# Delta-rule inverse: 8x8 diagonal blocks by back substitution in place of two product levels

## The chip, the cores and the metric

The kernel runs on one core of one Trainium2 chip. The metric is device microseconds of one execution, the median of three runs.

## The reference

Four residual layers over x (512 tokens x 1024): a gated DeltaNet, a gated ConvFFN, a differential attention, a second ConvFFN, each followed by a LayerNorm. What matters here is the DeltaNet's chunked delta rule, for each of 8 heads of width 128:

```python
low = jnp.where(strict, jnp.einsum('nbhid,nbhjd->nbhij', kb, k) * decay, 0.0)
a_mat = low + jnp.eye(C, dtype=f32)
rhs = jnp.concatenate([v * beta[..., None], kb * jnp.exp(gc)[..., None]], -1)
sol = lax.linalg.triangular_solve(a_mat, rhs, left_side=True, lower=True, unit_diagonal=True)
```

Then a scan over the chunks updates the state S and gives the output o, which is RMS-normalized, gated and projected. The kernel works with chunks of 128 tokens (NT = 4 of them) and forms the inverse T of the unit lower triangular matrix explicitly.

## The kernel before

Every engine has its own instruction list, written out by hand; the lists meet in semaphores. `PE_AT`, `DVE_AT`, `ACT_AT` and `POOL_AT` number the events of one head on each engine, and `pe("kk")`, `dve("L")`, `act("DT")`, `pool("TT")` wait for them; `own(...)` on an engine waits for an earlier result of its own. The DeltaNet's heads run one after the other (`step`, once on each engine; heads 0 to 5 in a loop over pairs, 6 and 7 unrolled, 7 with `more=False`). The parity e of the head picks one of two sets of buffers and three PSUM banks `X(e, 0..2)`.

Large products have float32 accuracy by three single products of high and low halves (`block_products`: L1449, L1450, L1451). While TensorE works on head h it also projects head h+1: 4 weight chunks (gate, q, k, v) x 8 contraction blocks = 32 fill units of three matmuls of 512 columns. `fill(p0, p1)` lays them between the small products of the head. In head 7 the fill is the output product instead (`mixer_unit`, 6 matmuls, L1437 to L1439), 14 units spread over the same 32 places. Each weight chunk (512 KB by DMA into one of two `raw` slots) is split by ScalarE (`split_hi`, L323) and VectorE (`split_lo`, L328) into one of four slots; `hold_hi` and `hold_lo` do it for the output weights kept aside. A raw slot is loaded again when its split is done.

The inverse T of a 128x128 block (four at once, one per chunk): L = k k^T scaled by the decays (L1083); T starts as the identity plus the negated sub-diagonal of the 2x2 blocks (VectorE L1085, L1087), its transpose TT the same from LT (GpSimd L552, L555). Then six levels s = 2, 4, 8, 16, 32, 64. In each, TensorE forms P = LT x T (`four`, L1505, 4 matmuls of 128 columns), VectorE masks it into PB (L1066), TensorE multiplies by TT for T's update and by PB for TT's (`part`, L1512, 4 matmuls of 64 columns each), and VectorE adds the updates (L1076, L1079). The last level updates TT alone. These products are in plain float32, for which the trace has two records per matmul. Between a level's first product and the others stand 2 fill units, 3 in level 2.

The order on TensorE in a head: 8 fill units, k k^T (event kk), k q^T (qk), k transposed (kt), 1 unit, L transposed (lt), 2 units, v transposed (vt, L1503, waits for `A`, the scaled q k^T, L1090), 1 unit, the levels, the recurrence over the four chunks with the state `S` (VectorE L1136, L1139) and the copies `v0` to `v3` (ScalarE), the last fill units, and the mean of squares (ms, L1593). Beside it ScalarE makes the decay factors DD, DT, ER (L682 to L689) from the row broadcast by a 256 KB DMA, and copies LT; GpSimd makes QD (L546), masks A (L549), then TTa and TT. VectorE does the convolution taps of the next head (`tap`, L1033, three per tensor, which free bank 0 or 1), the norms of q and k (L1041), and at the end o1, og, hi, lo of the finished head (L1150 to L1156).

Of the kernel before, what the change touches and what calls it, by code (L numbers as in the profile page):

```python
# [38 lines left out]
P = 128  # L39
# [20 lines left out]
LEVELS = [2, 4, 8, 16, 32, 64]  # L60
# [38 lines left out]
LV = [f"{k}{s}" for s in LEVELS for k in ("P", "T", "TT") if (k, s) != ("T", LEVELS[-1])]  # L99
PE_AT, PE_N = numbered(["kk", "qk", "kt", "lt", "vt"] + LV  # L100
                       + ["v0", "w", "S0", "v1", "S1", "v2", "S2", "v3", "o", "ms"])
DVE_AT, DVE_N = numbered(["L", "T0a", "T0", "A", "Rw", "kd", "Rv"] + LV + ["S0", "S1", "S2", "o1", "og", "hi", "lo"])
ACT_AT, ACT_N = numbered(["DDr", "DTr", "DD", "DT", "er", "LT", "v0", "w", "v1", "v2", "v3", "sq", "ln", "rms"])
POOL_AT, POOL_N = numbered(["qd", "mA", "TTa", "TT"])
# [24 lines left out]
def build(nc, a):  # L129
    ctx = ExitStack()  # L130
    with ctx:
# [24 lines left out]
        level = sb("level", [P, 7, P])  # L156
        level1T = sb("level1T", [P, P])
# [200 lines left out]
        def _(sp):  # L358
# [120 lines left out]
        def _(pool):  # L479
# [26 lines left out]
            made(nc.gpsimd.memset(level[:, :, :], 0.0))  # L506
            for i, s in enumerate([1] + LEVELS):

                v = level[:, i, :].rearrange("p (b h j) -> p b h j", h=2, j=s)[:, :, 0, :]
# [3 lines left out]
            made(nc.gpsimd.memset(level1T[:, :], 0.0))  # L513
            select(level1T[:, :].rearrange("p (b h) -> p b h", h=2)[:, :, 1], ALU.not_equal, -1.0, 0,
                   [[-2, P // 2]], 1)

# [19 lines left out]
            with pool.Fori(0, PAIRS) as it:  # L536
                for e in BOTH:
                    h = 2 * it + e
                    own = 1 + h * POOL_N
# [56 lines left out]
        def _(act):  # L596
# [73 lines left out]
            def step(h, e, more):  # L670
# [8 lines left out]
                act.wait_ge(row_loaded, 16 * h + 16)  # L679
# [15 lines left out]
                if more:  # L695
                    gate(h + 1, 1 - e)
                split_hi(act, C_GDN_IN, h, 7)
# [22 lines left out]
                if more:  # L720
                    split_hi(act, C_GDN_IN, h, 9)
                    tap(h + 1, 3)
# [19 lines left out]
            split_hi(act, C_GDN_IN, 0, 5)  # L742
            tap(0, 3)
# [179 lines left out]
        def _(dve):  # L923
# [56 lines left out]

            dve.wait_ge(params_loaded, 16 * N_PARAMS)
# [61 lines left out]

            def step(h, e, more):
# [49 lines left out]
                pe("vt")  # L1094
                nc.vector.tensor_tensor(RV[e][:, :, :], v3(X(e, 1)), bc(beta), ALU.mult).then_inc(d_dve, 1)
                split_lo(dve, C_GDN_IN, h, 6)
                if not more:
                    split_lo(dve, C_GDN_IN, h, 7)
                masked(0)
                added(0)  # L1100
                if more:
                    split_lo(dve, C_GDN_IN, h, 7)
                else:
                    hold_lo(dve, C_GDN_OUT + 4)
                masked(1)
                if more:
                    tap(h + 1, 1, 0)
                added(1)
                if more:
                    tap(h + 1, 1, 1)  # L1110
                masked(2)
                if more:
                    tap(h + 1, 1, 2)
                added(2)
                if not more:
                    hold_lo(dve, C_GDN_OUT + 5)
                masked(3)
                added(3)
                masked(4)
                added(4)  # L1120
# [4 lines left out]
                masked(5)  # L1125
                added(5)
# [811 lines left out]
```

## Time and profile before

| | us |
|---|---|
| median of 3 runs (lowest, highest) | 1574.72 (1572.68, 1575.71) |
| profiled execution: its time, its span | 1572.31, 1570.5 |
| busy in the span: PE, DVE, ACT, POOL | 1469.8, 869.2, 626.1, 130.3 |
| heads of the delta rule, first k k^T to the last ms | 67.47 to 481.18 |
| starts of k k^T in heads 0, 1, 6, 7 | 67.47, 118.08, 377.33, 435.11 |

The profile is of one execution. A row of busy time by stretch lists PE, PEld, DVE, ACT and POOL in this order. PE is the matrix engine (TensorE), PEld its weight loads, DVE VectorE, ACT ScalarE, POOL GpSimd. Matmuls overlap, so the distance between two starts tells what one costs, not its duration. A row's bracket says how long the engine was idle before it and what it waited for. "Clock" is the share of TensorE's full clock that was granted.

### The profile page before, as it was taken

To read this page: it belongs to the slowest core of one execution; us is meant where nothing else is said; L and a number is where in the kernel's file an instruction comes from. 1 tells how busy PE (TensorE), PEld (TensorE's weight loads), DVE (VectorE), ACT (ScalarE), POOL (GpSimd) and SP (SyncE) were. 2 spreads that over 40 slices of the span, in tenths; PEclk is the share of its full clock that TensorE was granted. 3 is DMA by queue.
4 is the path that set the end of the run, shared out by engine and by line. 5 is a ranking of instruction groups with operands and counts; after the bars stand their busy time and mean duration, and the time that the engine had idled before them with its cause. 6 is when DMAs were issued, how large, how long until landed. Compare 5 with 4: busy or idle time off the path is not lost.

```text
span 1570.5 us, 20997 instructions
## 1 busy us (share of the span) xinstructions
PE 1469.8 (94%) x7474; PEld 1204.3 (77%) x7474; DVE 869.2 (55%) x1288; ACT 626.1 (40%) x997; POOL 130.3 (8%) x121
## 2 busy tenths in 40 slices
PE   6899999999889699999999999999996999999997
PEld 5688778887777678888788777677676788887886
DVE  5556655666455466666522544777755666665225
ACT  4743554345422244444411224565522444444220
POOL 4101110111012000000000201111020000000002
PEclk8999999999999899999999999999998999999999
DMA  5211111111120133333322131112211333333321
GB/s 165 57 52 48 47 46 40 47 47 47 41 68 14 54 95 95 104 93 93 134 101 101 44 104 54 41 54 80 83 38 54 97 96 101 93 93 134 107 95 67
DMA packets 157726, 118.85 MB, mean 76 GB/s; under 512 B 5898, under 2 KB 145644, under 8 KB 157676
## 3 DMA queue, kind: packets, MB, share of 16 engines
q1 hardware_dynamic: 157676, 118.17, 24.6%
q8 instruction: 33, 0.54, 0.1%
q14 instruction: 17, 0.14, 0.0%
HBM read 116.04 MB, written 2.11 MB: 75 GB/s over the span
## 4 chain that ended last, share of the span: by engine, by line
PE 76%; DVE 10%; ACT 5%; issue 4%; POOL 2%; DMA 2%; SPq 1%; ACTq 0%; DVEq 0%; POOLq 0%
PE bank L1449 13%; PE bank L1451 13%; PE bank L1450 13%; PE bank L1437 7%; PE bank L1439 7%; PE bank L1438 7%; PE bank L1512 5%; PE bank L1505 3%; DVE w_lo L328 1%; PE bank L1787 1%; PE bank L1805 1%; DVE x_tok L1184 1%; PE bank L1746 1%; DVE bn L1188 1%; DVE x_tok L1199 1%
## 5 line engine op out<-in xcount | busy, mean ns | idle before, releaser
L1449 PE MATMUL bank<-x_hi,w_hi 128*128 128x512 f32 (+1 forms) x1160 | 463.3, 399 | 29.3 <-DVE x_lo L938 25.8
L1451 PE MATMUL bank<-x_hi,w_lo 128*128 128x512 f32 (+1 forms) x1160 | 442.3, 381 | 0.0
L1450 PE MATMUL bank<-x_lo,w_hi 128*128 128x512 f32 (+1 forms) x1160 | 441.7, 381 | 0.0
L328 DVE TENSOR_TENSOR w_lo<-raw,w_hi 128x1024 fp32r<-128x1024 f32 x196 | 246.6, 1261 | 311.6 <-ACT w_hi L323 298.9
L1449 PEld LDWEIGHTS bank<-x_hi,w_hi 128*128 128x128 f32 x1160 | 223.4, 193 | 68.4 <-DVE w_lo L328 24.2
L323 ACT ACTIVATE w_hi<-raw 128x1024 fp32r<-128x1024 f32 x188 | 196.9, 1050 | 191.9 <-PE bank L1439 154.3
L1451 PEld LDWEIGHTS bank<-x_hi,w_lo 128*128 128x128 f32 x1160 | 222.4, 192 | 41.5
L1450 PEld LDWEIGHTS bank<-x_lo,w_hi 128*128 128x128 f32 x1160 | 223.5, 193 | 37.3 <-issue 3.4
L1437 PE MATMUL bank<-w_hi,u_hi 128*128 128x512 f32 x416 | 165.9, 399 | 14.3 <-issue 5.7
L1439 PE MATMUL bank<-w_hi,u_lo 128*128 128x512 f32 x416 | 163.7, 393 | 0.0
L1438 PE MATMUL bank<-w_lo,u_hi 128*128 128x512 f32 x416 | 163.5, 393 | 0.0
L1437 PEld LDWEIGHTS bank<-w_hi,u_hi 128*128 128x128 f32 x416 | 79.1, 190 | 33.6 <-issue 11.3
L1439 PEld LDWEIGHTS bank<-w_hi,u_lo 128*128 128x128 f32 x416 | 79.0, 190 | 16.8
L1438 PEld LDWEIGHTS bank<-w_lo,u_hi 128*128 128x128 f32 x416 | 79.1, 190 | 16.5 <-issue 0.5
L564 POOL TENSOR_TENSOR x_tok<-x_tok,gb 128x1024 f32<-128x1024 f32 x8 | 19.3, 2408 | 854.3 <-DVE x_tok L1204 854.3
L823 ACT ACTIVATE u_hi<-acc_b 128x512 f32 (+1 forms) x44 | 27.8, 632 | 116.0 <-DVE acc_b L1277 116.0
L650 ACT ACTIVATE scr<-bank,vec 128x512 f32<-128x512 f32 x24 | 16.4, 684 | 116.7 <-PE bank L1451 116.7
L1033 DVE SCALAR_TENSOR_TENSOR scr<-bank,vec,scr 128x511 f32<-128x511 f32 (+2 forms) x72 | 53.6, 745 | 9.3 <-ACT scr L650 5.4
L820 ACT ACTIVATE acc_a<-acc_a 128x512 f32<-128x512 f32 x44 | 27.8, 632 | 77.6 <-DVE acc_a L1272 77.6
L1269 DVE SCALAR_TENSOR_TENSOR acc_b<-bank,vec,acc_b 128x511 f32<-128x511 f32 x44 | 33.0, 749 | 39.0 <-ACT acc_b L816 39.0
L816 ACT ACTIVATE acc_b<-bank,vec 128x512 f32<-128x512 f32 x44 | 34.2, 777 | 49.7 <-PE bank L1451 49.7
L1280 DVE TENSOR_TENSOR u_lo<-acc_b,u_hi 128x512 f32 (+1 forms) x44 | 30.5, 692 | 39.9 <-ACT u_hi L823 39.9
(268 smaller groups left out, 1925.6 us busy)
## 6 DMA issues: line engine op xcount, KB each, us to landing
raw<-in_ffn_w_up SPq DMA_DIRECT2D x88, 512.0 KB, 3.7
raw<-in_ffn_w_down SPq DMA_DIRECT2D x44, 512.0 KB, 3.2
raw<-in_gdn_w_in SPq DMA_DIRECT2D x32, 512.0 KB, 4.1
raw<-in_diff_w_in SPq DMA_DIRECT2D x24, 512.0 KB, 3.7
raw<-in_gdn_w_out SPq DMA_DIRECT2D x8, 512.0 KB, 3.3
raw<-in_diff_w_out SPq DMA_DIRECT2D x8, 512.0 KB, 3.3
x_tok<-in_x SPq DMA_DIRECT2D x4, 512.0 KB, 5.7
ROW<-decay_rows SPq DMA_DIRECT2D x8, 256.0 KB, 4.6
```

The costliest lines, as they stand in the source:

```text
L323: nc.scalar.activation(w_hi[:, s, :], raw[:, (base + r) % RAW, :], ACT.Copy).then_inc(hi_ready, 1)
L328: nc.vector.tensor_tensor(w_lo[:, s, :], raw[:, (base + r) % RAW, :], w_hi[:, s, :].bitcast(F32), ALU.subtract).then_inc(lo_ready, 1)
L816: nc.scalar.activation(acc, b[:, :], ACT.Identity, bias=fcb(l, t), scale=fcw(l, 2, t)).then_inc(f_act, 1)
L1033: ins = nc.vector.scalar_tensor_tensor(acc[:, sh:T], bank[r % 2][:, 0:T - sh], gcw(3 - sh, i * 8 + h), acc[:, sh:T], ALU.mult, ALU.add)
L1437: nc.tensor.matmul(out, hi[:, k, tok], high[:, cols], start=(k == 0), stop=False)
L1438: nc.tensor.matmul(out, hi[:, k, tok], low[:, cols], start=False, stop=False)
L1439: ins = nc.tensor.matmul(out, lo[:, k, tok], high[:, cols], start=False, stop=(k == K - 1))
L1449: nc.tensor.matmul(out, hi, x_hi[:, k, cols], start=(k == 0), stop=False)
L1450: nc.tensor.matmul(out, hi, x_lo[:, k, cols], start=False, stop=False)
L1451: ins = nc.tensor.matmul(out, lo, x_hi[:, k, cols], start=False, stop=last)
L1505: ins = nc.tensor.matmul(out, lhsT(n), rhs(n), start=True, stop=True)
L1512: ins = nc.tensor.matmul(halves(X(e, i)[:, c], s, h), lhsT[e][:, n, :], halves(rhs[e][:, n, :], s, h), start=True, stop=True)
```

## The change

The lowest levels are replaced by a direct solve. T's 8x8 diagonal blocks are found by back substitution: L is masked to its 8x8 diagonal blocks with a minus sign (`Lb`), a reduction packs the 16 blocks of a row into 8 columns (`Lc`, 128 x 4 x 8), a broadcast product with `place_in` (which column in its block a partition has) lays row m of each block in its own 8 columns (`R`, 128 x 256), and one float32 product with `same` (ones where two tokens share a block) spreads each row to all partitions of its block (`bc`, 256 columns, into bank `X(1-e, 2)`). VectorE then solves for m = 7 down to 1 in 13 small operations on `Tc` (128 x 4 x 8), and a last one writes T (`T0`). TT comes from T by four transposes on TensorE (`tt`) and a copy on ScalarE. Levels 2 and 4 and GpSimd's TTa and TT are gone. v is transposed behind level 8's first product, into `X(1-e, 2)`. The fill is cut anew: 7, 2, 2, 5, 1, 2 units, then as before. The weight splits move: each head does chunks 7 to 10 counted from its own first one, instead of 6 to 9; chunk 6 is split before head 0, and chunks 9 and 10 earlier in the head, ahead of the third tap. Head 7's second output unit no longer waits for all of head 6 but for its event `ln`. The row loads get a semaphore per parity.

```diff
-LEVELS = [2, 4, 8, 16, 32, 64]
+BASE = 8
+NB = P // BASE
+LEVELS = [8, 16, 32, 64]
...
@@ VectorE, before the heads
+            dve.wait_ge(masks_ready, 2)
+            nc.vector.tensor_reduce(place_in[:, :], ident[:, :].rearrange("p (b j) -> p j b", j=BASE), AX.X,
+                                    ALU.add).then_inc(place_ready, 1)
...
+            split_lo(dve, C_GDN_IN, 0, 6)
             norms(0, 0)
...
@@ GpSimd, in a head
-                    pool.wait_ge(d_act, from_act + ACT_AT["LT"])
-                    nc.gpsimd.tensor_tensor(TT[e][:, :, :], LT[e][:, :, :], rep(level1T[:, :]),
-                                            ALU.mult).then_inc(d_pool, 1)
-                    pool.wait_ge(d_pool, own + POOL_AT["TTa"])
-                    nc.gpsimd.tensor_tensor(TT[e][:, :, :], TT[e][:, :, :], rep(ident[:, :]),
-                                            ALU.add).then_inc(d_pool, 1)
...
@@ ScalarE, in a head
                 nc.scalar.activation(LT[e][:, :, :], v3(X(e, 0)), ACT.Copy).then_inc(d_act, 1)
-                split_hi(act, C_GDN_IN, h, 6)
                 if more:
+                    split_hi(act, C_GDN_IN, h, 7)
                     gate(h + 1, 1 - e)
-                split_hi(act, C_GDN_IN, h, 7)
+                    tap(h + 1, 1)
+                pe("tt")
+                nc.scalar.activation(TT[e][:, :, :], v3(X(e, 1)), ACT.Copy).then_inc(d_act, 1)
...
                 if more:
-                    tap(h + 1, 1)
                     silu(h + 1, 1 - e, 1)
                     split_hi(act, C_GDN_IN, h, 8)
+                    split_hi(act, C_GDN_IN, h, 9)
                     tap(h + 1, 2)
+                    split_hi(act, C_GDN_IN, h, 10)
...
                 if more:
-                    split_hi(act, C_GDN_IN, h, 9)
                     tap(h + 1, 3)
...
+            split_hi(act, C_GDN_IN, 0, 6)
             tap(0, 3)
...
@@ VectorE, the solve
+                rows_of = X(1 - e, 2)[:, 0:NT * BASE * BASE].rearrange("p (n m j) -> p n m j", m=BASE, j=BASE)
+                dve.wait_ge(d_pe, 1 + h * PE_N + PE_AT["bc"])
+                nc.vector.scalar_tensor_tensor(Tc[:, :, :], rows_of[:, :, BASE - 1, :], place_in[:, BASE - 1:BASE],
+                                               place_in[:, :].unsqueeze(1).to_broadcast([P, NT, BASE]), ALU.mult,
+                                               ALU.add).then_inc(d_dve, 1)
+                before = "c0"
+                for m in range(BASE - 2, 0, -1):
+                    own(before)
+                    nc.vector.tensor_tensor(step_c[:, :, 0:m], rows_of[:, :, m, 0:m],
+                                            Tc[:, :, m:m + 1].to_broadcast([P, NT, m]), ALU.mult).then_inc(d_dve, 1)
+                    own(f"c{m}")
+                    nc.vector.tensor_tensor(Tc[:, :, 0:m], Tc[:, :, 0:m], step_c[:, :, 0:m], ALU.add).then_inc(d_dve, 1)
+                    before = f"a{m}"
...
@@ VectorE, in a head
-                own("T0a")
-                nc.vector.tensor_tensor(TM[e][:, :, :], TM[e][:, :, :], rep(ident[:, :]), ALU.add).then_inc(d_dve, 1)
+                own("Lb")
+                nc.vector.tensor_reduce(Lc[:, :, :], TM[e][:, :, :].rearrange("p n (b j) -> p n j b", j=BASE), AX.X,
+                                        ALU.add).then_inc(d_dve, 1)
+                own("Lc")
+                nc.vector.tensor_tensor(spread(e), Lc[:, :, :].unsqueeze(2).to_broadcast([P, NT, BASE, BASE]),
+                                        place_in[:, :].unsqueeze(1).unsqueeze(3).to_broadcast([P, NT, BASE, BASE]),
+                                        ALU.mult).then_inc(d_dve, 1)
                 pe("qk")
                 act("DT")
                 nc.vector.tensor_tensor(AT[e][:, :, :], v3(X(e, 1)), DT[e][:, :, :], ALU.mult).then_inc(d_dve, 1)
+                if not more:
+                    split_lo(dve, C_GDN_IN, h, 7)
+                solve(h, e)
+                own(SOLVE[-1])
+                nc.vector.tensor_tensor(TM[e][:, :, :].rearrange("p n (b j) -> p n b j", j=BASE),
+                                        Tc[:, :, :].unsqueeze(2).to_broadcast([P, NT, NB, BASE]),
+                                        same[:, :].rearrange("p (b j) -> p b j", j=BASE).unsqueeze(1).to_broadcast(
+                                            [P, NT, NB, BASE]), ALU.mult).then_inc(d_dve, 1)
...
+                masked(0)
                 nc.vector.tensor_tensor(KD[e][:, :, :], v3(X(e, 2)), bc(kdecs), ALU.mult).then_inc(d_dve, 1)
...
                 if more:
                     split_lo(dve, C_GDN_IN, h, 7)
+                    tap(h + 1, 1, 0)
+                added(0)
+                pe("vt")
+                nc.vector.tensor_tensor(RV[e][:, :, :], v3(X(1 - e, 2)), bc(beta), ALU.mult).then_inc(d_dve, 1)
+                if not more:
                     hold_lo(dve, C_GDN_OUT + 4)
...
@@ TensorE
-                                pe.wait_ge(d_act, 1 + (HEADS - 1) * ACT_N)
-                                pe.wait_ge(d_dve, D_DVE0 + (HEADS - 1) * DVE_N)
+                                pe.wait_ge(d_act, 1 + (HEADS - 2) * ACT_N + ACT_AT["ln"])
...
-                dve("A")
-                pe.wait_ge(in_act, 1 + IA_N * h + IA["v silu"])
-                four(1, cols(vT), None, turn=True)
-                fill(11, 12)
-                p = 12
+                dve("R")
+                nc.tensor.matmul(X(1 - e, 2)[:, 0:NT * BASE * BASE], same[:, :], TT[e][:, 0:2, :].rearrange("p a b -> p (a b)"),
+                                 start=True, stop=True).then_inc(d_pe, 1)
+                fill(11, 16)
+                p = 16
...
                     four(0, at(LT), at(TM))
...
                     if i == 0:
+                        four(1, at(TM), None, turn=True)
+                        fill(p, p + 1)
+                        p += 1
+                        pe.wait_ge(in_act, 1 + IA_N * h + IA["v silu"])
...
+                    fill(p, p + 2)
+                    p += 2
                     if i == 0:
-                        pool("TT")
-                        dve("Rv")
+                        dve("kd")
+                        act("TT")
```

## Rows read from the trace of the kernel before

**Rows 1.** Busy us by stretch: start:end, length, engines (instructions), clock, DMA share, GB/s.

```profile
67.47:118.08 50.61, 49.68 (x308) 41.75 (x309) 27.50 (x44) 23.80 (x44) 6.14 (x4) 1.00 0.18 47
169.85:221.79 51.94, 49.74 (x310) 41.61 (x309) 30.30 (x46) 24.07 (x45) 5.97 (x4) 1.00 0.17 45
377.33:422.36 45.03, 43.14 (x283) 36.66 (x282) 25.09 (x39) 17.67 (x33) 5.97 (x4) 1.00 0.12 42
422.36:435.11 12.75, 8.20 (x22) 5.44 (x21) 7.05 (x10) 11.46 (x23) 1.28 (x1) 0.73 0.12 41
435.11:481.18 46.07, 40.44 (x274) 35.64 (x272) 22.62 (x33) 9.61 (x14) 4.65 (x3) 1.00 0.21 69
```

**Rows 2.** Order of time, TensorE, head 2: start, us, engine, line, names, [idle].

```profile
171.64 0.60 PE L1503 MATMUL bank<-ident,kT 128*128 128x128 f32 x4
171.99 0.48 PE L1449 MATMUL bank<-x_hi,w_hi 128*128 128x512 f32 x1
...
175.82 0.65 PE L1503 MATMUL bank<-ident,vT 128*128 128x128 f32 x4 [1.05 <-DVE DT L1090]
...
180.65 1.10 PE L1512 MATMUL bank<-PB,TT 128*128 128x64 f32 x8 [0.52 <-POOL TT L555]
...
186.80 1.11 PE L1505 MATMUL bank<-TM,LT 128*128 128x128 f32 x8
187.67 0.47 PE L1449 MATMUL bank<-x_hi,w_hi 128*128 128x512 f32 x1
...
189.13 1.00 PE L1512 MATMUL bank<-PB,TT 128*128 128x64 f32 x8
...
190.86 1.11 PE L1505 MATMUL bank<-TM,LT 128*128 128x128 f32 x8
...
194.93 1.08 PE L1467 MATMUL bank<-sq_q,ones 128*128 128x512 f32 x2
195.85 1.05 PE L1505 MATMUL bank<-TM,LT 128*128 128x128 f32 x8
```

**Rows 3.** Order of time, VectorE, start of head 2.

```profile
172.67 0.69 DVE L1085 TENSOR_TENSOR TM<-DD,level 128x512 f32<-128x512 f32 x1
173.40 1.69 DVE L1087 TENSOR_TENSOR TM<-TM,ident 128x512 f32<-128x512 f32 x1
175.01 0.68 DVE L1090 TENSOR_TENSOR DT<-bank,DT 128x512 f32<-128x512 f32 x1
175.61 0.67 DVE L1092 TENSOR_TENSOR RW<-bank,bege 128x512 f32<-128x512 f32 x1
```

**Rows 4.** Order of time, GpSimd, the same stretch.

```profile
173.24 1.30 POOL L546 TENSOR_TENSOR QD<-qT,ER 128x512 f32<-128x512 f32 x1 [44.57 <-ACT ER L689]
175.77 1.29 POOL L549 TENSOR_TENSOR DT<-DT,upto 128x512 f32<-128x512 f32 x1 [1.23 <-DVE DT L1090]
```

**Rows 5.** Order of time, ScalarE, the same stretch.

```profile
171.73 1.26 ACT L689 ACTIVATE ER<-ROW,gmid 128x128 f32<-128x128 f32 x4
```

**Rows 6.** Order of time, VectorE's small operations before the heads.

```profile
35.65 0.19 DVE L987 TENSOR_TENSOR ab<-ab,heads_row 128x32 f32<-128x32 f32 x1
35.88 0.19 DVE L990 SCALAR_TENSOR_TENSOR ab<-ab 128x32 f32<-128x32 f32 x1
...
44.14 0.19 DVE L1004 COPY gcol<-bank 128x32 f32<-128x32 f32 x1 [2.72 <-ACT kdecs L640]
...
44.96 0.29 DVE L1016 TENSOR_REDUCE small<-lamp 128x2 f32<-128x128 f32 x1
```

**Rows 7.** Order of time, TensorE, at both ends of the heads.

```profile
67.47 1.16 PE L1505 MATMUL bank<-kT 128*128 128x128 f32 x8 [0.95 <-DVE kT L1041]
...
426.99 0.47 PE L1437 MATMUL bank<-w_hi,u_hi 128*128 128x512 f32 x1 [3.50 <-DVE scr L1033]
...
442.66 0.50 PE L1437 MATMUL bank<-w_hi,u_hi 128*128 128x512 f32 x1 [2.90 <-DVE w_lo L328]
```

**Rows 8.** The page's costliest groups: VectorE's weight split.

```profile
L328 DVE TENSOR_TENSOR w_lo<-raw,w_hi 128x1024 fp32r<-128x1024 f32 x196 | 246.6, 1261 | 311.6 <-ACT w_hi L323 298.9
```

More of the change, by code:

```diff
@@ L155, in build @@
         after = sb("after", [P, P])
-        level = sb("level", [P, 7, P])
-        level1T = sb("level1T", [P, P])
+        level = sb("level", [P, len(LEVELS) + 1, P])
+        same = sb("same", [P, P])
+        place_in = sb("place_in", [P, BASE])
+        Lc = sb("Lc", [P, NT, BASE])
+        Tc = sb("Tc", [P, NT, BASE])
+        step_c = sb("step_c", [P, NT, BASE])
         ones = sb("ones", [P, P])
@@ L505, in _ @@
             made(nc.gpsimd.memset(mean_h[:, :], 1.0 / P))
-            made(nc.gpsimd.memset(level[:, :, :], 0.0))
-            for i, s in enumerate([1] + LEVELS):
-                v = level[:, i, :].rearrange("p (b h j) -> p b h j", h=2, j=s)[:, :, 0, :]
+            made(nc.gpsimd.memset(same[:, :], 1.0))
+            v = same[:, :].rearrange("p (b j) -> p b j", j=BASE)
+            select(v, ALU.is_ge, 0.0, 0, [[-BASE, NB], [0, BASE]], 1)
+            select(v, ALU.is_ge, 0.0, BASE - 1, [[BASE, NB], [0, BASE]], -1)
+            made(nc.gpsimd.memset(level[:, 0, :], -1.0))
+            v = level[:, 0, :].rearrange("p (b j) -> p b j", j=BASE)
+            select(v, ALU.is_gt, 0.0, 0, [[-BASE, NB], [-1, BASE]], 1)
+            select(v, ALU.is_ge, 0.0, BASE - 1, [[BASE, NB], [0, BASE]], -1)
+            made(nc.gpsimd.memset(level[:, 1:, :], 0.0))
+            for i, s in enumerate(LEVELS):
+                v = level[:, i + 1, :].rearrange("p (b h j) -> p b h j", h=2, j=s)[:, :, 0, :]
                 made(nc.gpsimd.memset(v, -1.0))
@@ L538, in _ @@
                     h = 2 * it + e
-                    own = 1 + h * POOL_N
                     from_act = 1 + h * ACT_N
@@ L1042, in norms, with spread, solve, own @@
                                                    ALU.mult, ALU.mult).then_inc(in_dve, 1)
+            def spread(e):
+                return TT[e][:, 0:2, :].rearrange("p a (b m j) -> p (a b) m j", m=BASE, j=BASE)
+            def solve(h, e):
+                def own(name):
+                    dve.wait_ge(d_dve, D_DVE0 + h * DVE_N + DVE_AT[name])
+                rows_of = X(1 - e, 2)[:, 0:NT * BASE * BASE].rearrange("p (n m j) -> p n m j", m=BASE, j=BASE)
[11 more added lines that the diff above has]
+                    before = f"a{m}"
             def step(h, e, more):
@@ L1106, in step @@
                 if more:
-                    tap(h + 1, 1, 0)
+                    tap(h + 1, 1, 1)
                 added(1)
                 if more:
-                    tap(h + 1, 1, 1)
+                    tap(h + 1, 1, 2)
+                else:
+                    hold_lo(dve, C_GDN_OUT + 5)
                 masked(2)
[L1112 to L1120, printed above, removed]
                 if more:
@@ L1124, in step @@
                     hold_lo(dve, C_GDN_OUT + 6)
-                masked(5)
-                added(5)
+                added(2)
+                if more:
+                    split_lo(dve, C_GDN_IN, h, 9)
+                masked(3)
+                added(3)
                 if not more:
@@ L1136, in step @@
                         nc.vector.tensor_copy(S, new).then_inc(d_dve, 1)
+                        if more:
+                            split_lo(dve, C_GDN_IN, h, 10)
                     else:
@@ L1167, in _ @@
                 tap(0, 3, j)
+            split_lo(dve, C_GDN_IN, 0, 6)
             norms(0, 0)
+            dve.wait_ge(place_ready, 1)
+            dve.wait_ge(masks_ready, N_MASKS)
             with dve.Fori(0, PAIRS - 1) as it:
@@ L1522, in step @@
                 pe.wait_ge(d_dve, 1 + h * DVE_N)
-                fill(0, 8)
+                fill(0, 7)
                 pe.wait_ge(in_dve, 1 + ID_N * h + ID["k norm"])
@@ L1527, in step @@
                 four(2, cols(kT), None, turn=True)
-                fill(8, 9)
+                fill(7, 9)
                 dve("L")
@@ L1555, in step @@
                     part(2, PB, TT, s, 1)
-                    if more and s == LEVELS[3]:
+                    if more and s == LEVELS[2]:
                         square_sum(h + 1, 1 - e, 0)
```

46 lines of the change are left out of this document (21 added, 25 removed).

## The prediction

> **What bounds the kernel now.** I read the busy times by stretch first [rows 1]. The eight heads of the delta rule are the stretch from 67.47 to 481.18 us. Heads 1 to 5 take (377.33 - 118.08) / 5 = 51.85 us each, with TensorE busy 49.74 of 51.94 and its clock at 1.00; VectorE is busy 30.30, ScalarE 24.07, GpSimd 5.97. So a head costs what TensorE does in it (the head's small products, and 32 units of the next head's projection laid between them), plus short waits. TensorE's order of time [rows 2] gives the prices. K is the start of the products k k^T: 169.85 in the head shown. Four transposes cost 0.35 (171.64 to 171.99). One level costs 0.87 for LT x T (186.80 to 187.67) and 1.73 for its two halved products (189.13 to 190.86), so 2.60 without fill; two fill units between take 1.46, which is 0.78 for the first and 0.70 for each further one. Two waits stand out: 1.05 modelled before the v transposes (1.22 against an undisturbed pitch) and 0.52 modelled (0.68) before the first halved product, put down to GpSimd's TT. The VectorE, GpSimd and ScalarE rows [rows 3 to 5] show where they come from: ScalarE's exponentials ER end at 172.99, GpSimd's QD runs 173.24 to 174.54, VectorE's second mask step on T (L1087) has 0.69 us of work, yet occupies 173.40 to 175.09, that is until QD ends plus its own time; the scaled q k^T follows and then the v transposes. I read this as: a VectorE operation with two SBUF inputs and a GpSimd one exclude each other. In contrast L1092 (an input in PSUM) runs 0.67 beside GpSimd's 1.29 at 175.77.
>
> **TensorE, part by part.** Removed in each head: levels 2 and 4, 2 x 2.60 = 5.20. Gone with them: 1.22 before the v transposes (they move behind level 8's first product, where v has long been ready), 0.68 for GpSimd's TT, and 0.15 in level 4. Added: four transposes for TT, 0.35; and the product that spreads the rows. It has 256 columns. The square sum, same type, 512 columns, takes 0.92 (194.93 to 195.85 [rows 2]), so 0.46 and some 0.1 for the change of weights; bounds 0.46 and 0.92. The number of fill units stays 32, cut into 16 pieces instead of 17 (-0.08). Without new waits: 51.85 - 5.20 - 1.22 - 0.68 - 0.15 - 0.08 + 0.35 + 0.56 = 45.45.
>
> **The new waits.** I walk one head from K. K comes one unit (0.70) earlier against the ScalarE chain from the head before, as 7 units precede it and not 8; the third tap now stands ahead of the weight split, which gives 0.16 back. So ER ends at K + 3.14 + 0.54 = 3.68 and QD runs 3.93 to 5.23. TensorE: kk, qk and k transposes to 2.14, two units to 3.62, L transposes to 3.97, two units to 5.45: there it wants R, the spread operand. VectorE: L starts near 2.2, Lb 2.9, Lc 3.65, at the dependent pitch of 0.72 [rows 3]. Lc, a reduction of 512 elements, isn't in the trace; the 128-element one takes 0.29 [rows 6], so 384 elements more at the pace of the 512-element products give 0.65 to 0.7; upper bound 1.69, what L1087 took with GpSimd in its way. I take 0.7. R reads two SBUF tensors and waits for QD's end: 5.23 to 5.6. TensorE loses 0.2 (bounds 0 and 1.2) and starts the spread at 5.65, fill at 6.2, and its five units end at 9.8.
>
> Meanwhile VectorE scales q k^T (5.6 to 6.2) and GpSimd masks it from 0.76 after that start (175.01 to 175.77 [rows 3, 4]): 6.36 to 7.65. The spread's result is there at about 6.5, 0.84 after its start. Now the solve: 13 dependent small operations on at most 32 elements. The nearest rows [rows 6]: 128x32, dependent, 35.65 to 35.88, pitch 0.23 at a duration of 0.19; read from PSUM also 0.19. The operations shrink to 4 elements, so I take 0.22 each; bounds 0.15 (the duration less its elements) and 0.35 (a quarter more than the 128-element reduction's 0.29). c0 and c6 read PSUM and run to 6.94; a6 reads two SBUF tensors and waits for GpSimd until 7.65; eleven more end near 10.05; the product that writes T0 takes 0.69, so T0 stands at 10.75. TensorE waited 0.95 for it (bounds: 0 if nothing waits for GpSimd and the operations take 0.19; 2.6 at 0.35 each). A pitch that differs by 0.1 moves each head by 1.3.
>
> The Trainium skill speaks against this form: "VectorE: DVE Perf Modes", section "The TRN2 errata — SBUF-src ops pay a fixed extra latency per instruction", gives each instruction a fixed cost, which many small tiles pay each time, and 62 cycles (65 ns) more for a PSUM source. By it the seven operations that read the spread rows cost 0.45 a head more and the kernel would end 3.6 later, near 1537; the row of the 32-element copy from PSUM (0.19, as from SBUF) doesn't agree, and I go by the row. The same skill's "SBUF — State Buffer", section "Who interferes with whom", has tensor_reduce never contend with GpSimd; if the trace holds otherwise, QD starts up to 0.4 late behind Lc and so does the rest; no row of before shows a long reduction.
>
> **The rest of a head.** Level 8 starts at x = K + 10.75. VectorE does RW (0.6), level 8's mask (from x + 1.15), KD to x + 2.4; ScalarE's copy of TT is done by x + 2.1; TensorE has 0.87 + 0.35 + 0.78 + 0.35 + 1.48 = 3.8 before it needs them: hidden. The split of chunk 7 and the first tap end by x + 4.2, before the T8 product ends. Further on the covers are thinner: the split of chunk 8 waits for ScalarE, which now does the silu and square of the new q just before; it ends near x + 14.5, and T32's addition stands behind it, wanted at x + 14.55. I charge 0.3; bounds 0 and 1.5 (both splits late by one 1.2). The splits of chunks 9 and 10 move before and behind S0, whose waits in the trace are VectorE waiting for TensorE. Each head still issues four 512 KB loads and one 256 KB row, now in some 46.7 us instead of 51.9: 51 GB/s instead of 45 [rows 1]. The row load of two heads on is queued behind load 12 and waits for v3 of this head, while the next weight load wants a split of the next head: nothing is held. GpSimd loses TTa and TT, which also frees the split that they slowed. Sum: 45.45 + 0.2 + 0.95 + 0.3 = 46.9; the walk, by 10.75 to level 8 and 35.96 from there to the next K, has 46.7. I take 46.7, a gain of 5.15.
>
> **The ends.** Head 0 (50.61 [rows 1]) lacked the 1.22, but ER is early, so neither R nor a6 waits: 45.85, gain 4.75. Head 6 up to its mean of squares: 45.03 becomes 40.5, gain 4.5. The passage to head 7, 12.75, has a 3.50 wait for the taps [rows 7], then a wait for head 6's last instruction, and a clock of 0.73. The taps now run before the split (1.2 earlier) and the second wait is only for ScalarE's logarithm. So 3.4, and three units of the output product at 1.39: 7.6, gain 5.2, at full clock. Head 7 (46.07): -5.20 for the levels, -2.9 for the split that TensorE waited for [rows 7], +0.91 for the added products, +0.9 for T0, +1.4 for the first held weight split, which VectorE now reaches behind TT8 and RV, when TensorE has used its fill: gain 5.0. Against this, the split of chunk 6 moved ahead of head 0: VectorE has k normalized at 67.41, TensorE waited 0.95 for it [rows 7]; one split of 1.26 [rows 8] and ScalarE's own stand before it now. Bounds 1.1 and 2.3, I take 1.6. That makes TensorE idle for 3.1 there; behind the idle 3.5 at 423.5 the clock fell, with 13 matmuls 0.2 longer each. I charge one such fall, 2.6 (bounds 0 and 5.2, for one at either end). The reduction for place_in stands in the chain of gates at 35 us: 0.25.
> Sum: 4.75 + 5 x 5.15 + 4.5 + 5.2 + 5.0 - 1.6 - 2.6 - 0.25 = 40.75. The profiled execution took 1572.31 (span 1570.5); the median of the three others is 2.4 higher. 1574.72 - 40.75 = 1534.0. All after 481 us (1,089 us) is not touched.
>
> **The rivals.** (a) The solve is hidden: operations at 0.19, the GpSimd mask out of the way, no clock fall. 1.15 a head and 2.6: 1534.0 - 9.2 - 2.6 = 1522. For it: VectorE is idle 20 us in a head. Against: the mask's start is tied to VectorE's own product just before. 12 in 100. (b) The small operations cost 0.35: 13 x 0.13 = 1.7 a head, 1547.5. For it: seven of them read a strided PSUM pattern with a broadcast, which no row shows. Against: the durations barely depend on the size. 17 in 100. (c) VectorE's queue becomes the limit inside the levels, as each addition that TensorE wants stands behind a split or a tap: 1.2 a head more, 1543.5. The first levels of before show that 0.15 is lost behind a split. 10 in 100. (d) Slower: the wait before T0 makes the clock fall in every head. The idle 3.5 did that, 1.05 a head doesn't. From 0.42 an operation the wait is 3.5 and the fall costs 2.6 more, which together is the whole gain of a head; at 0.50 it is 3.6 + 2.6 = 6.2 a head, and the time 1584. Speaks against it: no small operation of the trace is near. 3 in 100. That the levels' products stay isn't possible: they are issued in one list. My forecast has 58 in 100.
>
> **Numbers.** Range 1523 to 1550: it takes in (a) but for its edge, (c) and (b). Faster by over 0.2% (3.1 us, about what can be told from no change here) 0.95, within it 0.02, slower 0.03.
>
> **What would show it.** Right: from K to K 46.7, some 270 matmuls a head in place of 310; R ends just after QD; a6 long, about 0.9, and its eleven followers near 0.22 apart; TensorE's wait before level 8 about 1 us; no wait before the v transposes. Wrong: a wait of 2 or more before level 8 or a clock under 1.00 inside the heads (b, d); waits before levels 16 to 64 put down to T (c); the start of head 0's products earlier than 68.5 or later than 70.5.

## The result: 1530.3 us, 44 us less, and the profile after

The changed kernel's median is 1530.31 us (four runs, 1526.78 to 1533.51) beside 1574.45 before; the ratio is 0.972 with a 95% interval of 0.9696 to 0.9744. Forecast were 1534.0 and a range of 1523 to 1550. The profiled execution took 1530.73, its span is 1529.0 instead of 1570.5: 41.5 less. All of it lies in the heads: the last mean of squares starts at 439.56 instead of 481.18, 41.6 earlier, and the rest takes 1089.4 as against 1089.3.

Busy us by stretch after the change (columns as in [rows 1]): head 0, head 4, head 6 to its mean of squares, the passage to head 7, and head 7.

```profile
70.57:117.89 47.32, 46.49 (x266) 38.81 (x267) 27.52 (x52) 23.64 (x41) 2.62 (x2) 0.96 0.24 67
256.76:303.12 46.36, 44.98 (x267) 37.21 (x266) 30.24 (x56) 24.94 (x45) 2.60 (x2) 1.00 0.19 51
349.36:389.75 40.39, 39.17 (x245) 32.77 (x243) 26.08 (x49) 19.78 (x35) 2.59 (x2) 1.00 0.16 53
389.75:398.79 9.04, 6.79 (x21) 4.85 (x21) 6.01 (x9) 8.54 (x20) 0.00 (x0) 0.81 0.00 1
398.79:439.56 40.77, 36.22 (x231) 31.13 (x230) 21.13 (x41) 11.16 (x18) 3.47 (x2) 1.00 0.21 65
```

Against [rows 1]: head 0 has 47.32 instead of 50.61; heads 1 to 5 (117.89 to 349.36) have 46.29 on average instead of 51.85; then 40.39 for 45.03, 9.04 for 12.75, 40.77 for 46.07. TensorE has 44.98 busy of 46.36 in head 4 and 267 matmul records instead of 310. VectorE's busy time is as before (30.24): what it lost in levels it got back in the solve. GpSimd's falls from 5.97 to 2.60, with two operations left of four. The clock stays at 1.00 inside head 4; it is under 1 in head 0 and in the passage.

TensorE in head 4, from the spread product (L1583) to level 64, answering to [rows 2]:

```profile
262.28 0.70 PE L1583 MATMUL bank<-TT,same 128*128 128x256 f32 x2
262.63 0.58 PE L1500 MATMUL bank<-x_hi,w_hi 128*128 128x512 f32 x1
...
267.10 1.16 PE L1555 MATMUL bank<-TM,LT 128*128 128x128 f32 x8 [0.67 <-DVE TM L1140]
268.09 0.60 PE L1553 MATMUL bank<-ident,TM 128*128 128x128 f32 x4
268.45 0.47 PE L1500 MATMUL bank<-x_hi,w_hi 128*128 128x512 f32 x1
...
269.23 0.60 PE L1600 MATMUL bank<-ident,vT 128*128 128x128 f32 x4
...
280.89 1.08 PE L1518 MATMUL bank<-sq_q,ones 128*128 128x512 f32 x2
282.04 1.16 PE L1555 MATMUL bank<-TM,LT 128*128 128x128 f32 x8
```

The same stretch on VectorE and on GpSimd, answering to [rows 3, 4]. L1127 is the packing reduction, L1130 the spread operand R, L1072 c0, L1078 the products and L1081 the additions of the solve, L1140 writes T0.

```profile
260.29 1.13 DVE L1127 TENSOR_REDUCE Lc<-TM 128x32 f32<-128x512 f32 x1
261.45 0.78 DVE L1130 TENSOR_TENSOR TT<-Lc,place_in 128x256 f32<-128x256 f32 x1
262.15 0.68 DVE L1135 TENSOR_TENSOR DT<-bank,DT 128x512 f32<-128x512 f32 x1
263.02 0.25 DVE L1072 SCALAR_TENSOR_TENSOR Tc<-bank,place_in 128x32 f32<-128x32 f32 x1 [0.19 <-PE bank L1583]
263.31 0.18 DVE L1078 TENSOR_TENSOR step_c<-bank,Tc 128x24 f32<-128x24 f32 x1
263.52 0.73 DVE L1081 TENSOR_TENSOR Tc<-Tc,step_c 128x24 f32<-128x24 f32 x1
264.29 0.18 DVE L1078 TENSOR_TENSOR step_c<-bank,Tc 128x20 f32<-128x20 f32 x1
...
266.15 0.17 DVE L1081 TENSOR_TENSOR Tc<-Tc,step_c 128x4 f32<-128x4 f32 x1
266.35 0.69 DVE L1140 TENSOR_TENSOR TM<-Tc,same 128x512 f32<-128x512 f32 x1
```

```profile
260.65 1.29 POOL L561 TENSOR_TENSOR QD<-qT,ER 128x512 f32<-128x512 f32 x1 [42.78 <-ACT ER L698]
262.91 1.30 POOL L564 TENSOR_TENSOR DT<-DT,upto 128x512 f32<-128x512 f32 x1 [0.96 <-DVE DT L1135]
```

Read the first addition of the solve: 0.73 us at 263.52, the next ones 0.18. It ends at 264.25, 0.04 behind the end of GpSimd's mask (262.91 + 1.30 = 264.21). R (L1130) takes 0.78 where QD (L561) is still running until 261.94. Since the solve ends late, T0 stands at 267.04. TensorE's last fill unit begins at 265.58, and at 0.68 for a unit the next product could have started at 266.26; it starts at 267.10. So TensorE loses 0.84, of which the row shows 0.67.

### The profile page after: what moved, and what is told of

Its sections match the earlier page's. It is cut to its first block, busy times and chain, and to the rows that moved or that the text cites. A ratio compares the mean times of both kernels' runs of the same rounds, so it can differ in the third digit from the quotient of the medians.

```text
span 1529.0 us, 20387 instructions
## 1 busy us (share of the span) xinstructions
PE 1430.5 (94%) x7138; PEld 1168.3 (76%) x7138; DVE 870.0 (57%) x1361; ACT 632.2 (41%) x1005; POOL 100.4 (7%) x100
## 4 chain that ended last, share of the span: by engine, by line
PE 79%; DVE 13%; ACT 3%; issue 2%; DMA 2%; SPq 1%; DVEq 0%; ACTq 0%
PE bank L1500 14%; PE bank L1502 14%; PE bank L1501 14%; PE bank L1488 7%; PE bank L1490 7%; PE bank L1489 7%; PE bank L1555 3%; PE bank L1562 2%; DVE w_lo L340 1%; PE bank L1845 1%; PE bank L1863 1%; PE bank L1804 1%; DVE x_tok L1235 1%; DVE bn L1239 1%; DVE x_tok L1250 1%
## 5 line engine op out<-in xcount | busy, mean ns | idle before, releaser
L340 DVE TENSOR_TENSOR w_lo<-raw,w_hi 128x1024 fp32r<-128x1024 f32 x196 | 239.7, 1225 | 304.8 <-ACT w_hi L335 292.4
L837 ACT ACTIVATE u_hi<-acc_b 128x512 f32 (+1 forms) x44 | 27.8, 632 | 116.0 <-DVE acc_b L1328 116.0
L834 ACT ACTIVATE acc_a<-acc_a 128x512 f32<-128x512 f32 x44 | 27.8, 632 | 78.0 <-DVE acc_a L1323 78.0
L830 ACT ACTIVATE acc_a<-bank,vec 128x512 f32<-128x512 f32 x44 | 34.2, 778 | 23.4 <-PE bank L1502 23.4
```

The source lines that it names most:

```text
L340: nc.vector.tensor_tensor(w_lo[:, s, :], raw[:, (base + r) % RAW, :], w_hi[:, s, :].bitcast(F32), ALU.subtract).then_inc(lo_ready, 1)
L830: nc.scalar.activation(acc, b[:, :], ACT.Identity, bias=fcb(l, t), scale=fcw(l, 2, t)).then_inc(f_act, 1)
```

## The experiments

Twelve experiments ran, one of them the changed kernel again. For those that ran several times the ratio is to the kernel before. A profile's total also varies outside the heads: from the last mean of squares to the end, code that no kernel touches, it is 1089.2 to 1094.6 in the fourteen profiles. So for one edit I go by the distance from one head's k k^T to the next's, which differs by 0.1 within a profile, and by the times only where they are many.

**1. GpSimd's mask behind the solve.**

```diff
-                    pool.wait_ge(d_dve, D_DVE0 + h * DVE_N + DVE_AT["A"])
+                    pool.wait_ge(d_dve, D_DVE0 + h * DVE_N + DVE_AT["T0"])
```

> The changed kernel, but GpSimd masks the scaled q k^T only when T0 is written. Theory (two-input VectorE operations and GpSimd's exclude each other): the first addition a6 falls from 0.73 to 0.18 us, so T0 is ready 0.55 earlier and TensorE's wait before level 8 falls from 0.67 modelled to about 0.1; from one head's k k^T to the next's 45.7 to 45.8 instead of 46.28; about 4.4 us in all. The mask then runs beside operations that read PSUM and is done before the next weight split. Rival (a6 is long for another reason, as the first addition or by its size): a6 stays at 0.73, heads stay at 46.28, time unchanged.

Heads take 45.69 to 45.82. The time is 1525.89 (four runs), ratio 0.9704 (0.9678 to 0.9730); the interval overlaps the changed kernel's, the heads don't. The additions of the solve, VectorE then GpSimd:

```profile
260.73 0.18 DVE L1078 TENSOR_TENSOR step_c<-bank,Tc 128x24 f32<-128x24 f32 x1
260.94 0.18 DVE L1081 TENSOR_TENSOR Tc<-Tc,step_c 128x24 f32<-128x24 f32 x1
261.16 0.18 DVE L1078 TENSOR_TENSOR step_c<-bank,Tc 128x20 f32<-128x20 f32 x1
```

```profile
264.00 1.27 POOL L564 TENSOR_TENSOR DT<-DT,upto 128x512 f32<-128x512 f32 x1 [4.63 <-DVE TM L1140]
```

The first addition is like the others. The theory holds and the rival falls.

**2 and 3. A longer solve.** Each product is issued three or five times, which leaves its result as it is.

```diff
-SOLVE = ["c0"] + [f"{k}{m}" for m in range(BASE - 2, 0, -1) for k in "ca"]
+SOLVE = ["c0"] + [f"{k}{m}" for m in range(BASE - 2, 0, -1) for k in [*(f"x{i}_" for i in range(AGAIN)), "c", "a"]]
```

> The changed kernel, with each of the six products of the solve issued three times (same result), so 25 small operations instead of 13. Theory (the solve lies on the path, its operations cost 0.21 each): 12 x 0.21 = 2.5 us a head more, the wait before level 8 becomes 3.2, heads 48.8, some 20 us in all, and no clock fall inside the heads. Rival (the solve is mostly hidden by fill and the wait has another cause): under 1 us a head. Rival d of the prediction (a long wait before level 8 lets the clock fall): granted clock under 1.00 in the heads and more than 3.5 us a head.

> The same with each product issued five times: 37 small operations. Theory: 24 x 0.21 = 5.0 us a head if the clock holds. The wait is then 5.7, longer than the 3.5 behind which the clock fell in the kernel before; so I expect a fall in each head, 13 to 15 matmuls 0.2 longer, 7.6 to 8 us a head, heads near 54, and so slower than the kernel before: about 1593. Rival (no fall, the clock goes by the whole head): 51.3 a head, 1571.

Two heads of the 25-operation kernel and the starts of their level 8, then two heads of the one with 37 and the start of level 8 in the second of them:

```profile
218.91:267.22 48.31, 44.86 (x268) 37.19 (x266) 31.80 (x68) 24.93 (x45) 2.60 (x2) 1.00 0.18 49
267.22:317.20 49.98, 46.56 (x268) 38.46 (x266) 31.86 (x67) 24.90 (x45) 2.58 (x2) 0.97 0.18 47
```

```profile
231.23 1.16 PE L1557 MATMUL bank<-TM,LT 128*128 128x128 f32 x8 [2.75 <-DVE TM L1142]
...
279.58 1.16 PE L1557 MATMUL bank<-TM,LT 128*128 128x128 f32 x8 [2.73 <-DVE TM L1142]
```

```profile
176.49:228.90 52.41, 46.58 (x268) 38.70 (x267) 33.85 (x80) 24.93 (x45) 2.59 (x2) 0.97 0.16 45
228.90:282.32 53.42, 47.59 (x267) 39.61 (x266) 33.75 (x80) 24.90 (x45) 2.60 (x2) 0.94 0.16 44
```

```profile
243.57 2.07 PE L1557 MATMUL bank<-TM,LT 128*128 128x128 f32 x8 [5.12 <-DVE TM L1142]
```

With 25 operations three of heads 1 to 5 take 48.31 to 48.37: 2.05 more for 12 operations. Twelve at 0.21 are 2.5; 0.42 of it is saved, as the first addition comes that much later and finds GpSimd further on (it takes 0.29 instead of 0.73). The time is 1552.1 in one run. The other two take 49.97 and 49.98, at a clock of 0.97, behind a wait of the same length (2.73 and 2.75). So a fall costs 1.65 there. I had expected none at this length; one length of wait gives both outcomes. With 37, heads 1 to 5 have 52.37 to 53.67 behind waits of 5.1 to 5.3, and the clock is never 1.00 but 0.97 or 0.94. In those heads level 8's first product already takes 1.97 to 2.08 us, so the clock is down when the wait ends; with 25 operations it takes 1.16 in all five heads, and where the clock falls, it does so behind it. From the first operation of the solve to T0 the 37 take 7.76 (235.06 to 242.82) and the 13 take 3.33 (263.02 to 266.35). Without a fall a head would have 46.29 + 4.43 = 50.7, so a fall costs 1.7 to 3.0. I had taken more for the longer operations and the fall together, and so the kernel took 1582.4 (one run) and not 1593. It is slower than the one before (1572.4 beside it): the prediction's slower case exists. But spread over the 13 operations, the 25 amount to 0.41 each (5.39 in all) and the 37 to 0.60, and at 0.41 a head still gains 1.9 to 3.5; I had put the point where the gain is gone at 0.42, so that case was further off than I had it.

**4. The packing reduction, in order of address.** This kernel leaves the packing out, so what it computes is no longer the inverse; it serves to price the reading alone.

```diff
-                nc.vector.tensor_reduce(Lc[:, :, :], TM[e][:, :, :].rearrange("p n (b j) -> p n j b", j=BASE), AX.X,
+                nc.vector.tensor_reduce(Lc[:, :, :], TM[e][:, :, :].rearrange("p n (j b) -> p n j b", j=BASE), AX.X,
```

> The changed kernel, with the reduction that packs the blocks reading its 512 elements in order of address (16 neighbours to a sum) instead of 16 elements 32 bytes apart; this leaves the packing out, so the inverse isn't the reference's. Strided reading as the cause of 1.1 us: falls to 0.7, as the 128-element one by its 0.29 in order and 0.38 strided. Rival (a reduction costs by its element count and groups alike): stays at 1.1. In both the heads keep 46.28, since the spread operand waits for GpSimd's QD.

One line's instructions (ns min/median/max), the changed kernel and this one:

```profile
L1127 DVE TENSOR_REDUCE Lc<-TM x8: 1093/1127/1189, 73.3 to 401.3; 128x32 f32<-128x512 f32 x8
```

```profile
L1127 DVE TENSOR_REDUCE Lc<-TM x8: 686/686/689, 72.8 to 397.6; 128x32 f32<-128x512 f32 x8
```

686 ns in order, 1127 strided by 32 bytes. The heads stay at 46.24 to 46.31 (1527.05 in one run), since R waits for QD in any case. The 0.7 that I had taken is the price of reading in order.

**5. The kernel before with GpSimd's work in another order**: TTa and TT, then the mask, QD last (four blocks moved, TensorE's wait for the last of them renamed).

> The kernel before with one edit: GpSimd does TTa and TT first, then the mask of A, and QD last. Theory (two of the terms of the forecast, 1.22 before the v transposes and 0.68 before the first halved product, belong to GpSimd's place in the head and not to the levels): L1087 falls from 1.69 to 0.69, the wait before the v transposes and the one for TT go, 1.3 to 1.9 us a head, heads 50.0 to 50.5 instead of 51.85, and 10 to 14 us in all, 1560. So about a third of the changed kernel's gain was to be had without the solve. Rival (those waits are put down wrongly and come from ScalarE's chain): they stay, under 3 us in all. Bounds for the case that QD, now last, becomes late for the recurrence: a wait at the product with QD, no gain.

Head 3 and head 7; VectorE's second mask step, TensorE's v transposes:

```profile
219.73:270.29 50.56, 49.68 (x309) 41.63 (x308) 28.80 (x46) 24.09 (x45) 5.90 (x4) 1.00 0.18 47
428.43:475.57 47.14, 41.74 (x274) 36.62 (x273) 22.38 (x33) 9.61 (x14) 6.99 (x4) 0.96 0.23 68
```

```profile
223.25 0.69 DVE L1087 TENSOR_TENSOR TM<-TM,ident 128x512 f32<-128x512 f32 x1
```

```profile
224.90 0.66 PE L1503 MATMUL bank<-ident,vT 128*128 128x128 f32 x4 [0.25 <-ACT vT L656]
```

Heads 1 to 5 take 50.39 to 50.58, 1.33 less, as expected, and L1087 has its 0.69. In all, though, the ratio is only 0.997 (0.9957 to 0.9984; ten runs, 1569.99 beside 1573.39), 3 to 5 us and not 10 to 14: I had multiplied by eight. In the profile heads 0 to 6 gain 8.5, but head 0 starts 1.12 later, the passage, which keeps its wait of 3.5, takes 13.48 instead of 12.75 at a clock of 0.62 instead of 0.73, and head 7 takes 47.14, 1.07 more than before, at a clock of 0.96. So 1.3 of a head's 5.56 was to be had without the solve.

**6. Six fill units ahead of level 8.**

```diff
-                fill(11, 16)
-                p = 16
+                fill(11, 17)
+                p = 17
```

(and one unit instead of two behind the v transposes)

> The changed kernel with six fill units instead of five between the spread product and level 8, one fewer behind the v transposes. Theory: the unit (0.70) covers the wait of 0.67 before level 8; the place it leaves needs KD and TT only 2.4 us after level 8's start and has 3.1 left; heads 45.6 to 45.7 instead of 46.28. Rival (TensorE then waits for KD or TT): heads 46.0 to 46.3 with a wait before level 8's first halved product.

```profile
252.14:297.78 45.64, 44.94 (x267) 37.20 (x266) 30.21 (x55) 24.92 (x45) 2.58 (x2) 1.00 0.19 52
```

Heads 1 to 5 take 45.55 to 45.64 (1524.4 in one run). The unit covers the wait and is free where it was taken from: the theory holds.

**7. Chunk 6's split behind head 0's norms.**

```diff
-            split_hi(act, C_GDN_IN, 0, 6)
             tap(0, 3)
             norm_exp(0, 0)
             norm_exp(0, 1)
+            split_hi(act, C_GDN_IN, 0, 6)
```

(and on VectorE, `split_lo` behind `norms`)

> The changed kernel with chunk 6's split behind the norms of head 0 on both engines instead of ahead of the third tap and of the norms. Theory: k is normalized 1.1 to 1.5 earlier, the wait before head 0's first products falls from 3.17 to 1.7 to 2.1. At that length the clock may hold (it fell behind 2.75 in two of five heads of the 25-operation kernel and held behind 1.05), which would make head 0 45.8 to 46.3 instead of 47.32. Rival (ScalarE's decay factors, one split later now, are then the last in head 0): L waits for DD, a wait before the L transposes of up to 1.

The first product of head 0, the changed kernel and this one, and this one's head 0:

```profile
70.57 1.16 PE L1555 MATMUL bank<-kT 128*128 128x128 f32 x8 [3.17 <-DVE kT L1058]
```

```profile
66.27 1.16 PE L1555 MATMUL bank<-kT 128*128 128x128 f32 x8 [1.69 <-DVE kT L1058]
```

```profile
66.27:112.82 46.55, 45.16 (x266) 37.29 (x267) 29.62 (x53) 25.12 (x46) 2.61 (x2) 1.00 0.25 69
```

The wait is 1.69 instead of 3.17, the clock 1.00, head 0 takes 46.55 instead of 47.32. L did wait for ScalarE (1.08 on VectorE), hidden by fill. Head 7's mean of squares starts 4.86 earlier than in the first profile of the changed kernel, and 1.66 earlier than in its second (experiment 10), where the clock fell neither at 54.7 nor in the passage. The one profile's total was 1530.0 all the same: its rest took 1093.6. The three kernels with this edit (7, 9 and 12) have the three longest rests, 1093.5 to 1094.6, the others 1089.2 to 1092.4; why, I haven't tried, so whether the edit itself gives some of its gain back there stays open.

**8. Blocks of 4 instead of 8**: `BASE = 4`, `LEVELS = [4, 8, 16, 32, 64]`, three fill units in place of five, two in the new level.

> The changed kernel with 4x4 diagonal blocks: a solve of 5 small operations, and level 4 back, with its two fill units. Theory (a level costs TensorE 2.60, the small operations only what they leave uncovered): + 2.60 for the level, - 0.1 to 0.2 for the narrower spread product (64 columns), and the wait before level 4 from 0.67 to 0.3 to 0.5, as 8 operations less (1.7) stand against two fill units less (1.4) and the mask of A still blocks: heads 48.4 to 48.8, some 19 us slower than the changed kernel. Rival (a dropped level is worth less than its products since other waits fill the place): heads under 47.8.

```profile
217.57:266.69 49.12, 47.26 (x291) 39.79 (x290) 30.56 (x50) 24.84 (x45) 2.60 (x2) 1.00 0.18 48
```

```profile
225.96 1.16 PE L1557 MATMUL bank<-TM,LT 128*128 128x128 f32 x8 [0.47 <-DVE TM L1140]
...
230.82 1.10 PE L1564 MATMUL bank<-PB,TT 128*128 128x64 f32 x8 [0.75 <-ACT TT L710]
```

49.1 to 49.3, 1552.0 in one run: 2.9 a head for the level, more than the 2.1 to 2.5 expected. The 0.47 before level 4 was expected; the 0.75 wasn't: ScalarE's copy of TT stands behind the tap of chunk 1, and chunk 1 is projected only with unit 16, which now comes later. The rival (under 47.8) falls. Without that 0.75, which comes of where the copy stands, the level would cost a head some 2.2 (an estimate from these rows), less than the 2.60 of its products, since the solve of 4x4 blocks is shorter and its spread product narrower. So what a dropped level is worth with the copy well placed isn't shown.

**9, 10 and 12. Edits 1, 6 and 7 together; the changed kernel again; and the three edits with QD behind T0 too.**

```diff
                     pool.wait_ge(in_dve, 1 + ID_N * h + ID["q norm"])
+                    pool.wait_ge(d_dve, D_DVE0 + h * DVE_N + DVE_AT["T0"])
```

> The changed kernel with three edits at once: the mask of A behind T0, six fill units ahead of level 8, chunk 6's split behind the norms. Each alone: heads 45.75, 45.58, and head 0's start 4.3 earlier (66.27). The first two hide the same wait, so heads 45.4 to 45.6, not 45.0; head 0 45.5 to 46, start 66.3 to 68.6. Sum against the changed kernel: 5 x 0.7 + 1 + 2 to 4, 6 to 9 us: 1521 to 1524. Rival (the gains of the start are lost again in the rest, as one profile had it): 1526.

> The changed kernel as it is, beside the one with three edits: 1530 plus or minus 2, ratio to before 0.972 to 0.974. Heads 46.3; the start and the passage to head 7 differ with the clock's falls by up to 2 us each.

> The three edits and GpSimd's QD behind T0 as well. Theory: R is no longer held (0.78 becomes 0.43), the spread product starts with TensorE's own pace, 0.08 to 0.15 earlier; with the mask ending 2.6 behind T0 the split of chunk 7 is held by some 0.2, covered. Heads 0.1 lower than with three edits. Rival (QD late for the recurrence or the split of chunk 7 holding up T8): heads higher by 0.2 or more.

```profile
249.12:294.52 45.40, 44.69 (x267) 37.26 (x266) 29.68 (x55) 24.96 (x45) 2.57 (x2) 1.00 0.19 52
379.20:388.35 9.15, 6.94 (x21) 4.92 (x21) 6.01 (x9) 8.64 (x20) 0.00 (x0) 0.81 0.00 1
```

```profile
248.38:293.56 45.18, 44.47 (x267) 37.34 (x266) 29.33 (x55) 24.91 (x45) 2.53 (x2) 1.00 0.20 52
377.91:385.42 7.51, 5.29 (x22) 3.78 (x22) 5.83 (x9) 7.01 (x15) 0.00 (x0) 1.00 0.00 1
```

```profile
253.06 0.43 DVE L1131 TENSOR_TENSOR TT<-Lc,place_in 128x256 f32<-128x256 f32 x1
...
254.96 0.18 DVE L1082 TENSOR_TENSOR Tc<-Tc,step_c 128x24 f32<-128x24 f32 x1
```

| kernel | heads 1 to 5 | head 0 | passage | time (runs) | ratio to before |
|---|---|---|---|---|---|
| changed, again | 46.23 to 46.36 | 47.36 | 7.51 | 1529.29 (5) | 0.9724 (0.9706 to 0.9742) |
| three edits | 45.29 to 45.41 | 45.56 | 9.15 | 1524.85 (5) | 0.9684 (0.9667 to 0.9702) |
| and QD | 45.17 to 45.21 | 45.24 | 7.51 | 1520.88 (1) | one run only |

The three edits give 4.4 by the medians; their interval doesn't touch the changed kernel's beside it. I had forecast 1521 to 1524, and 1526 if the rest took the gains of the start back; the 1524.85 lies between, with a rest of 1094.6 in its profile. With QD out of the way R takes 0.43 instead of 0.78, and the heads lose another 0.15. The last kernel has the lowest heads of all and one time only, so how it stands to the three edits isn't settled.

**11. The kernel before, with the shorter wait of head 7's second output unit.**

```diff
-                                pe.wait_ge(d_act, 1 + (HEADS - 1) * ACT_N)
-                                pe.wait_ge(d_dve, D_DVE0 + (HEADS - 1) * DVE_N)
+                                pe.wait_ge(d_act, 1 + (HEADS - 2) * ACT_N + ACT_AT["ln"])
```

> The kernel before with one edit: head 7's second output unit waits for head 6's logarithm and not for its last instruction. Theory: the second wait of the passage (1.04 modelled) goes, the 3.50 for the taps stays, and with it the fall of the clock: passage 11.3 to 11.7 instead of 12.75. Head 7 then reaches k k^T one unit earlier against VectorE's tail, and loses none of it. Rival (that wait is covered by the other): 12.7.

```profile
420.86:431.28 10.42, 6.91 (x21) 4.93 (x21) 7.06 (x10) 10.37 (x22) 0.65 (x1) 0.84 0.15 50
431.28:478.95 47.67, 42.02 (x274) 37.02 (x273) 22.63 (x33) 10.73 (x16) 5.28 (x4) 0.96 0.21 67
```

The passage takes 10.42 instead of 12.75, even less than expected, since the clock's fall was short (0.84). Head 7 then took 47.67 instead of 46.07, at a clock of 0.96, behind its unchanged 2.9 wait. The net gain is 0.7: what is saved by one wait can be lost again behind the next. The one run took 1570.9, within the range of the kernel before.

## Why the prediction was right, step by step

Two of the forecast's own sums are slightly off: the terms for TensorE come to 45.43, not 45.45, and 3.6 on top of 1534.0 make 1537.6, not 1537. Nothing hangs on them.

- **The levels' products, 5.20 a head.** Right. 43 records of matmuls went. From level 8's start to the next k k^T I had 35.96; measured 303.12 - 267.10 = 36.02.
- **The two waits that go, 1.22 and 0.68.** Right, and experiment 5 takes most of them away without the solve: 1.33 of 1.9, since the v transposes then wait 0.25 for ScalarE's v.
- **The spread product, 0.56.** Too high. It takes 0.35 to the next start (262.28 to 262.63), and the fill unit behind it has 0.88 instead of 0.78: 0.45.
- **The start of the walk.** Times are from the start of k k^T: QD predicted 3.93 to 5.23, measured 3.89 to 5.18; R's end 5.6, measured 5.47; the spread's start 5.65, measured 5.52. Level 8's start 10.75, measured 10.34.
- **The reduction, 0.7.** Wrong by 0.43 (1.13, within its bounds), without effect here: it ended at 261.42, QD at 261.94.
- **The solve, 13 at 0.22, the first addition held by GpSimd.** Right: starts 0.20 to 0.22 apart (0.29 behind c0), and a6, the first addition, 0.73 where I had about 0.89 (0.71 of waiting and its own 0.18). The wait before level 8 was 0.95 forecast and is 0.84. Products with an input in PSUM take 0.17 to 0.18 us, additions within SBUF the same, so the higher price for a PSUM source in the Trainium skill's "VectorE: DVE Perf Modes", section "The TRN2 errata — SBUF-src ops pay a fixed extra latency per instruction", doesn't show in them, as the forecast had it. One pair of rows leaves it open for another kind of operation: c0, a scalar_tensor_tensor of 32 elements from PSUM, takes 0.25, while L990's within SBUF takes 0.19 [rows 6]; whether the source or the different operands make the 0.06, no run tells.
- **The covers further on.** The 0.3 for T32 is 0.23 (280.89 + 0.92 to 282.04). No other wait came.
- **The passage, 5.2 gained.** It depends on the clock: 9.04 in the profile with a fall (0.81), 7.54 and 7.51 in experiments 1 and 10 without. Of the eleven profiles with the solve, four have a fall there (8.94 to 9.15) and seven have none (7.51 to 7.55). I had 7.6 without a fall and counted the one fall at the start.
- **The start, -1.6 and -2.6.** Head 0 started 3.10 later than before, where I had 1.85: the clock fell once more at 54.7, behind an idle of 1.96; before, an idle of 1.93 at this place had brought no fall. The 70.57 is also past the 70.5 that I had named as a sign of being wrong. Much of that is this one profile's own: head 0 starts at 68.42 to 70.57, 69.2 on average, in the eight profiles with the changed kernel's start, and at 65.85 to 68.59, 67.3 on average, in the three with the start of before, 1.85 apart. The idle before head 0 was 3.17 where I had 3.1, and the clock fell behind it as forecast. Head 0 gained 3.29 where I had 4.75 - 2.6 = 2.15, by two errors that cancel in part: without a fall (experiment 7) it takes 46.55 and not 45.85, since R and a6 then wait for GpSimd there too (0.87 and 0.73), and the fall costs 0.77 more and not 2.6.
- **Sum.** Forecast 40.75, measured 41.6 in the profiles. Forecast and measured gains by stretch: the start -1.85 and -3.10; head 0 with its fall 2.15 and 3.29; heads 1 to 5 25.75 and 27.8; head 6 4.5 and 4.64; the passage 5.2 and 3.71; head 7 5.0 and 5.30. By the medians the gain is 44.1, with an interval of 4 us to either side. The agreement of the total is in part luck, misses that cancel: the passage's fall, -1.5, and the later start, -1.25, against 0.41 in each of heads 1 to 5, 2.05 in all, and 1.1 in head 0.

Rival a (the solve all hidden) is what experiments 9 and 12 made of the kernel by further edits, 0.95 to 1.1 a head where I had 1.15. Rival b (slow operations) fell with the 0.21, rival c (VectorE late in the levels) with the single 0.23. Rival d (the clock falls in every head) was built as experiment 3.

## What to carry to other kernels

Where one engine is busy all the time, price a change by that engine's start-to-start distances and then walk its neighbours once through the stretch for the waits that appear; here that gave level 8's start to 0.4 us. Put GpSimd's work on SBUF where VectorE reads PSUM, or behind its chain of small operations, not beside it: each collision here cost the chain the rest of GpSimd's operation. And judge such edits by distances within a profile: the untouched rest of this kernel varies by 5 us between profiles.

## What the runs showed of the hardware

- VectorE's additions with two SBUF inputs don't run beside a GpSimd operation on SBUF, even at 24 elements: 0.73 instead of 0.18 (experiment 1). The Trainium skill, "SBUF — State Buffer", section "Who interferes with whom", states such a lock and that a reduction takes no part; the reduction here takes 1.11 us with GpSimd idle (experiment 12) and 1.13 beside QD, which agrees.
- A VectorE reduction with 16 elements 32 bytes apart takes 1.13 us for 512, in order of address 0.69.
- Dependent VectorE operations on 4 to 32 elements start 0.20 to 0.29 us apart, from PSUM or SBUF.
- The same wait of TensorE doesn't always bring the same clock: of five waits of 2.7 us in experiment 2, two were followed by a fall from 2.4 GHz (0.97 over the head against 1.00, 1.65 us more), three not. Behind the waits of 5.1 to 5.3 in experiment 3 it fell every time (0.94 to 0.97, 1.7 to 3.0 us more). A wait of 1.69 at head 0 brought none in experiment 7. Those of 2.67 and 2.92 in head 7 brought one in experiments 5 and 11 (0.96), the 2.90 of the kernel before none (1.00). The 2.2 in the passage brought one in four of eleven profiles (0.81, 1.4 to 1.6 us more).
